# A hybrid decoder step on one Trainium2 core: rotary features 32 partitions apart, and seven low halves of weights made on GpSimd

## What is computed

```python
def rms_norm(x, w):
    y = xf * lax.rsqrt(jnp.mean(xf * xf, axis=-1, keepdims=True) + EPS)
    return (y * w.astype(jnp.float32)).astype(x.dtype)

def partial_rope(x, pos):
    half = ROT_DIM // 2
    ...
    x1, x2 = xf[..., :half], xf[..., half:ROT_DIM]
    out = jnp.concatenate([x1 * cos - x2 * sin, x2 * cos + x1 * sin, xf[..., ROT_DIM:]], axis=-1)
...
    aq = partial_rope(rms_norm(aq.reshape(B, S, ATT_HEADS, ATT_HD), q_norm_w), pos)
    ak = partial_rope(rms_norm(ak.reshape(B, S, ATT_HEADS, ATT_HD), k_norm_w), pos)
```

## Time and profile before

| | before |
|---|---|
| median of 3 runs | 477.11 us (476.24 to 478.72) |
| profiled execution, its own time | 477.14 us |
| its span in the trace | 475.0 us |
| PE busy | 462.9 us (97%), weight loads 422.3 us (89%) |
| DVE busy | 403.4 us (85%) |
| ACT busy | 290.2 us (61%) |
| POOL busy | 101.8 us (21%) |

### The profile page before, as it was taken

One profiled execution on the slowest core, in us unless ns is written; L12 is line 12 of the kernel. 1 busy time (PEld: TensorE's weight loads), 2 busy tenths in 40 slices (PEclk: granted clock), 3 DMA queues, 4 the chain that ended last, 5 costly groups with the idle time before them and its releaser, 6 DMA issues.

```text
span 475.0 us, 11339 instructions
## 1 busy us (share of the span) xinstructions
PE 462.9 (97%) x3860; PEld 422.3 (89%) x3860; DVE 403.4 (85%) x1650; ACT 290.2 (61%) x486; POOL 101.8 (21%) x181
## 2 busy tenths in 40 slices
PE   6999999999989999999999999999999999999997
PEld 4899899998779898888899889899898898899997
DVE  4898899699999898999899999789999954567861
ACT  4866545666964584994485695657848368334430
POOL 2031321013223223422321332312223110000000
PEclk9999999999999999999999999999999999999999
DMA  8697589657999999999999999998999996446511
GB/s 310 257 392 290 211 307 339 219 200 246 313 418 409 412 366 322 337 398 414 413 386 352 386 398 393 417 383 309 344 420 410 415 412 213 172 172 236 186 79 47
DMA packets 36665, 150.86 MB, mean 318 GB/s; under 512 B 5232, under 2 KB 6772, under 8 KB 29312
## 3 DMA queue, kind: packets, MB, share of 16 engines
q1 hardware_dynamic: 12304, 70.77, 39.2%
q0 software_dynamic: 19008, 67.20, 37.1%
q10 hardware_dynamic: 5296, 12.18, 6.6%
HBM read 137.37 MB, written 12.76 MB: 316 GB/s over the span
## 4 chain that ended last, share of the span: by engine, by line
PE 72%; DVE 12%; ACT 9%; issue 3%; DMA 3%; ACTq 0%; SPq 0%; DVEq 0%
PE pj L533 26%; PE pj L536 13%; PE wk L533 8%; PE pa L726 5%; PE wk L536 4%; DVE w L1056 3%; DVE kpages L1155 3%; ACT w L812 2%; DMA out_C_s<-cslot 2%; DVE cslot L1243 2%; ACT L832 2%; PE wk L486 2%; PE wk L638 2%; PE wk L670 1%; DMA cst<-in_consts 1%
## 5 line engine op out<-in xcount | busy, mean ns | idle before, releaser
L533 PE MATMUL pj<-xn,w 128*128 128x264 f32 x1328 | 180.9, 289 | 0.4 <-ACT mqT L965 0.4
L533 PEld LDWEIGHTS pj<-xn,w 128*128 128x128 f32 x1328 | 168.5, 189 | 8.5 <-issue 6.8
L1056 DVE TENSOR_TENSOR w<-wraw,w 128x1024 fp32r<-128x1024 f32 x112 | 136.9, 1226 | 11.0 <-ACT w L812 10.5
L812 ACT ACTIVATE w<-wraw 128x1024 fp32r<-128x1024 f32 x112 | 117.8, 1053 | 25.2 <-PE wk L536 12.8
L1155 DVE CUSTOM_DVE_ANT_0 kpages<-kpages,qbc 128x128 f32<-128x128 f32 x512 | 114.7, 288 | 1.6 <-DMA kpages<-in_cache_k 1.4
L536 PE MATMUL pj<-xn,w 128*128 128x264 f32 x664 | 94.2, 284 | 3.7 <-DVE w L1056 3.7
L536 PEld LDWEIGHTS pj<-xn,w 128*128 128x128 f32 x664 | 85.5, 188 | 4.6 <-DVE w L1056 4.6
L403 POOL DMA_DIRECT2D kpages<-in_cache_k x64 | 34.3, 536 | 178.4 <-DVE sco L1155 154.6
L403 POOL DMA_DIRECT2D vpages<-in_cache_v x64 | 33.9, 529 | 67.2 <-issue 37.3
L1155 DVE DVE_READ_ACCUMULATOR2_ANT sco<- 128x1 f32 x512 | 41.7, 81 | 0.0
L726 PE MATMUL pa<-vpages,prob 128*32 128x256 f32 x512 | 34.3, 385 | 0.8 <-ACT prob L870 0.8
(11 more groups left out here) (279 smaller groups left out, 658.3 us busy)
## 6 DMA issues: line engine op xcount, KB each, us to landing
wraw<-in_weights SPq DMA_DIRECT2D x56, 1024.0 KB, 7.9
kpages<-in_cache_k POOLq DMA_DIRECT2D x64, 512.0 KB, 8.0
vpages<-in_cache_v POOLq DMA_DIRECT2D x64, 512.0 KB, 10.3
cslot<-in_states SPq DMA_DIRECT2D x16, 512.0 KB, 10.5
out_C_s<-cslot ACTq DMA_DIRECT2D x16, 512.0 KB, 8.0
xres<-in_tokens SPq DMA_DIRECT2D x1, 1056.0 KB, 7.2
out_k_p<-kT ACTq DMA_DIRECT2D x4, 256.0 KB, 11.6
out_v_p<-v_nat ACTq DMA_DIRECT2D x4, 256.0 KB, 6.5
```

Of the source, the lines that this page charges most:

```text
L533: mm(bank[:, 0:T], w2[:, q, 0, k, :], src[:, g, k, :], start=(k == 0 and g == 0), stop=False)
L812: A(w2[:, n % WSPLIT, 0], wraw[:, pair % WRAW, :, (n % 2) * P:(n % 2 + 1) * P], ACT.Copy).then_inc(whi_ready, 1)
L1056: V.tensor_tensor(w2[:, q, 1], wraw[:, slot, :, half * P:(half + 1) * P], w2[:, q, 0], ALU.subtract).then_inc(wlo_ready, 1)
```

## The change

The features of a query or key head are put in another order by permuting columns of the weights, the norm weights and the outputs: features 0 to 15 and 16 others on partitions 0 to 31, features 16 to 31 and 16 others on partitions 32 to 63, the rest above. Cosine is 1 and sine 0 for the features that aren't rotated; the sine carries the sign. DVE then multiplies partitions 32 to 63 by the sine and writes the product to partitions 0 to 31, and the other way round. PE's product with `rot` goes. Query rows, which have to come out in the old order, are made by matmuls with a permutation matrix (`back`) in place of transposes. The low halves of chunks 1 to 7 are made by POOL, with a semaphore of their own. Before the decay rows POOL does a broadcast of 8 numbers whose result nobody uses.

```diff
+        def low_ready(n):
+            return (own_lo_ready, n) if 1 <= n <= OWN else (wlo_ready, 1 if n == 0 else n + 1 - OWN)
...
             def load_w(n):
                 if n >= WRAW:
-                    sp.wait_ge(wlo_ready, 2 * (n - WRAW + 1))
+                    for half in range(2):
+                        sp.wait_ge(*low_ready(2 * (n - WRAW) + half))
...
+            def split_lo(n):
+                pool.wait_ge(own_lo_ready, n - 1)
+                pool.wait_ge(whi_ready, n + 1)
+                pool.tensor_tensor(w2[:, n % WSPLIT, 1], wraw[:, (n // 2) % WRAW, :, (n % 2) * P:(n % 2 + 1) * P], w2[:, n % WSPLIT, 0],
+                                   ALU.subtract).then_inc(own_lo_ready, 1)
+
+            pool.wait_ge(blank, 6)
+            for n in range(1, 4):
+                split_lo(n)
             pool.wait_ge(proj, 2)
             for s in range(KSLOTS):
                 keys(s)
+            split_lo(4)
             for s in range(VSLOTS - 1):
                 values(s)
+            for n in range(5, OWN + 1):
+                split_lo(n)
+
+            pool.wait_ge(own_lo_ready, OWN)
+            nc.gpsimd.partition_broadcast(gm[:, 0, :], qmask[0:1, 0, 0:HEADS]).then_inc(blank, 1)
+            pool.wait_ge(blank, 7)
             pool.wait_ge(rows_ready, 1)
...
-                pe.wait_ge(wlo_ready, n + 1)
+                pe.wait_ge(*low_ready(n))
...
-            def norm_sums(ss, ro, i, src):
-                mm(ss[:, 0:T], ones, sq[:, i, :], start=True, stop=True)
-                mm(ro[:, 0:T], rot, src, start=True, stop=True).then_inc(norm_ps, 1)
+            def norm_sums(ss, i):
+                mm(ss[:, 0:T], ones, sq[:, i, :], start=True, stop=True).then_inc(norm_ps, 1)
...
                     pe.wait_ge(evac, g + 1)
-                    if g == 0:
-                        pe.wait_ge(boot_r, 16)
                     if g >= 2:
-                        pe.wait_ge(q_ready, g - 1)
+                        pe.wait_ge(rs_ready, g - 1)
...
-                    last = tr(bank[0:NB, (h - first) * P:(h - first + 1) * P], qT[:, h, SEQ:T], P)
+                    last = mm(bank[0:NB, (h - first) * P:(h - first + 1) * P], qT[:, h, SEQ:T], back, start=True, stop=True)
...
-                        pe.wait_ge(attg_ready, 2 * j)
...
-                        pe.wait_ge(mrs_ready, j + 1)
...
-            for n in range(1, AHEAD):
-                split_lo(n)
-            def rope_norm(x, r, ro, done):
-                ch.step(V.tensor_tensor(hT[:, 0, :], ro[:, 0:T], sin, ALU.mult))
-                ch.link(V.tensor_tensor(x, x, cos, ALU.mult))
-                ch.link(V.tensor_tensor(x, x, hT[:, 0, :], ALU.add))
+            def rope_norm(x, r, done):
+                low, high, both = slice(0, LO), slice(LO, 2 * LO), slice(0, 2 * LO)
+                ch.step(V.tensor_tensor(hT[low, 0, :], x[high], sin[high], ALU.mult))
+                ch.step(V.tensor_tensor(hT[high, 0, :], x[low], sin[low], ALU.mult))
+                ch.link(V.tensor_tensor(hT[both, 1, :], x[both], cos[both], ALU.mult))
+                ch.link(V.tensor_tensor(x[both], hT[both, 0, :], hT[both, 1, :], ALU.add))
                 V.tensor_tensor(x, x, r, ALU.mult).then_inc(done, 1)
             for h in range(HEADS):
-                if h + AHEAD < HEADS + LOW:
+                if OWN < h + AHEAD < HEADS + LOW:
                     split_lo(h + AHEAD)
...
-                dve.wait_ge(norm_ps, h + 1)
                 dve.wait_ge(rs_ready, h + 1)
...
+ORDER = np.concatenate([np.arange(ROT // 2), np.arange(ROT, ROT + LO - ROT // 2), np.arange(ROT // 2, ROT),
+                        np.arange(ROT + LO - ROT // 2, HD)])
...
+    c[np.arange(P), C_BACK + ORDER] = 1.0
```

More of the change, by code:

```diff
@@ L66 @@
 JOBS = 4
+OWN = HEADS - 1
 BLANKS = 6
 C_ID, C_ONE, C_EPS, C_PICK, C_PICKB, C_FIRST = 0, 128, 256, 257, 273, 288
-C_ROT, C_MASK, C_TRIT, C_COS, C_SIN, C_RANK, C_END = (
+C_BACK, C_MASK, C_TRIT, C_COS, C_SIN, C_RANK, C_END = (
     288, 416, 800, 928, 928 + T, 928 + 2 * T, 928 + 2 * T + 32)
@@ L237, in build @@
         ones = cst[:, C_ONE:C_ONE + P]
-        rot = cst[:, C_ROT:C_ROT + P]
+        back = cst[:, C_BACK:C_BACK + P]
         mask3 = cst[:, C_MASK:C_MASK + 384]
@@ L281, in build @@
         wload = [sem(f"wload{i}") for i in range(WRAW)]
-        whi_ready, wlo_ready = sem("whi_ready"), sem("wlo_ready")
+        whi_ready, wlo_ready, own_lo_ready = sem("whi_ready"), sem("wlo_ready"), sem("own_lo_ready")
+        def low_ready(n):
+            return (own_lo_ready, n) if 1 <= n <= OWN else (wlo_ready, 1 if n == 0 else n + 1 - OWN)
         kload = [sem(f"kload{i}") for i in range(KSLOTS)]
@@ L572, in keys_side @@
                         pe.wait_ge(c_ready, NB * j - 2) if j else pe.wait_ge(q_ready, HEADS)
[L573 removed]
                     else:
                         pe.wait_ge(c_ready, NB * j) if j else pe.wait_ge(qs_ready, 2)
[L576 to L577 removed]
+                    norm_sums(wk[2 * n], n)
                 if i in (4, 6):
@@ L1115, in _ @@
                 dve.wait_ge(boot_r, 16)
-                dve.wait_ge(norm_ps, h + 1)
                 dve.wait_ge(rs_ready, h + 1)
-                rope_norm(qT[:, h, :], rs[:, h % 2, :], wk[2 * (h % 2) + 1], q_ready)
+                rope_norm(qT[:, h, :], rs[:, h % 2, :], q_ready)
                 dve.wait_ge(q_ready, h + 1)
@@ L1203, in keys_side @@
                     n = i // 2 - 1
-                    dve.wait_ge(norm_ps, HEADS + 2 * j + n + 1)
                     dve.wait_ge(rs_ready, HEADS + 2 * j + n + 1)
                     dve.wait_ge(mlg_ready, j)
-                    rope_norm(kT[:, n, :], rs[:, n, :], wk[2 * n + 1], kT_ready)
+                    rope_norm(kT[:, n, :], rs[:, n, :], kT_ready)
                     dve.wait_ge(kT_ready, 2 * j + n + 1)
@@ L1435, in constants @@
     half = ROT // 2
-    for m in range(half):
-        c[m + half, C_ROT + m] = -1.0
-        c[m, C_ROT + m + half] = 1.0
+    c[np.arange(P), C_BACK + ORDER] = 1.0
     r = np.arange(P)
@@ L1448, in constants @@
     for s in range(2):
-        c[s * half:(s + 1) * half, C_COS:C_COS + T] = np.cos(ang)
-        c[s * half:(s + 1) * half, C_SIN:C_SIN + T] = np.sin(ang)
+        c[s * LO:s * LO + half, C_COS:C_COS + T] = np.cos(ang)
+        c[s * LO:s * LO + half, C_SIN:C_SIN + T] = np.sin(ang) * (1 - 2 * s)
     c[:, C_RANK:C_RANK + 32] = 2 * BIG * (TOPK - 0.5 - np.repeat(np.arange(NBLK)[::-1], HEADS))[None, :]
@@ L1467, in weight_pairs @@
 def weight_pairs(w_in, w_proj_mlstm, w_proj_attn, w_out):
-    cuts = [w_in[:, AQ + 256 * n:AQ + 256 * (n + 1)] for n in range(4)]
-    cuts += [w_in[:, g + 256 * j:g + 256 * (j + 1)] for j in range(JOBS) for g in GROUPS]
+    pair = np.concatenate([ORDER, HD + ORDER])
+    cuts = [w_in[:, AQ + 256 * n + pair] for n in range(4)]
+    cuts += [w_in[:, g + 256 * j + (pair if g == AK else np.arange(256))] for j in range(JOBS) for g in GROUPS]
     for w in (w_in[:, GA:GA + D], w_in[:, GM:GM + D], w_proj_mlstm, w_proj_attn, w_out):
@@ L1495 @@
         "consts": constants(),
-        "columns": np.concatenate([cols(n) for n in ("norm_w", "q_norm_w", "k_norm_w", "mh_norm_w")], axis=1),
+        "columns": np.concatenate([cols("norm_w"), cols("q_norm_w")[ORDER], cols("k_norm_w")[ORDER], cols("mh_norm_w")], axis=1),
         "tokens": np.concatenate([np.ascontiguousarray(inputs["x_prompt"])[0], np.ascontiguousarray(inputs["x_sample"])[:, 0]]).T
@@ L1513 @@
     y = g["y"].reshape(P, KC, T).transpose(2, 1, 0).reshape(T, D)
-    k_p = g["k_p"].transpose(3, 0, 2, 1).reshape(rows)
+    there = np.argsort(ORDER)
+    k_p = g["k_p"][:, there].transpose(3, 0, 2, 1).reshape(rows)
     v_p = g["v_p"].reshape(JOBS, P, 2, 256).transpose(2, 1, 0, 3).reshape(rows)
@@ L1520 @@
     return (y[:SEQ].reshape(1, SEQ, D), y[SEQ:].reshape(NB, 1, D), k_p, v_p, C_p, g["n_p"], g["m_p"].reshape(1, 1, MH),
-            by_sample(g["k_s"]), by_sample(g["v_s"]), C_s, n_s, g["m_s"])
+            by_sample(g["k_s"][there]), by_sample(g["v_s"]), C_s, n_s, g["m_s"])
```

3 lines of the change are left out of this document (1 added, 2 removed).

## The result

The changed kernel takes 494.35 us (median of 4 runs, 492.64 to 495.34), the kernel before 477.92 us in the same runs: ratio 1.0348 [1.0326, 1.037], **+16.4 us**. The forecast was +5.8 with a range up to 488. The direction was right, the size was not. The profiled execution takes 493.83 us, its span is 492.1 us.

A forecast was written before the change was run, and what follows sets the result against it. PE was taken to bound the kernel nearly everywhere, with DVE close behind. 477.14 us plus 6.0 for the heads stage minus 0.2 for the body gave 482.9 us (+1.2%), range 474.5 to 488.0.

The forecast's parts named there:

- PE's products with `rot`: Sixteen fp32 products of 0.45 us go from PE: 3.6 us in the heads stage, 3.6 us in the body.
- time taken off PE counts: Premise that PE bounds nearly everywhere, so its savings count where DVE or a late half doesn't take them back.
- DVE's rotation: Five DVE instructions per head: 2.09 us against 1.73, 0.36 more; upper end 2.3 us, 0.57 more.
- A low half on POOL: One low half made by POOL takes 2.2 us, against 1.22 on DVE; ends 0.95 and 2.65 us.
- When half 5 is there: Heads stage: POOL's half 5, behind the value loads, comes at 36.5 us; PE wants it at 32.6 and waits 3.9.
- POOL and DVE hold each other up: Start of the heads stage: POOL's first half holds DVE's `x_lo` once, making PE and all behind it 2.0 us later.
- The end of the heads stage: Half 7 ends at 42.9 us, last `q_ready` comes at 53.7, next chunk starts at 55.9 instead of 49.9: +6.0 us.
- Query rows: End of the heads stage: fp32 matmuls of 0.22 us replace eight transposes of 0.11 us, 0.9 us more.
- The decay rows: POOL's decay rows start at about 44 us, are spread at 50 to 52, needed at 58: no cost.
- The body: Rounds after the heads stage: -0.9 in round 0, +0.36 each in rounds 1 and 2, 0 in round 3; sum -0.2 us.
- more held up: Rival: POOL comes in twice at the start, halves take 2.65 us, or body rotations cost their upper end; 485 to 489, chance 0.18.

The follow-up runs named there:

- rotation alone: The changed kernel with all low halves back on DVE in the old places and no unused broadcast; 485.94 us, ratio 1.0184.
- unread product: The rotation alone with one fp32 product of 264 columns more on PE ahead of each sum of squares, 16 in all, unread; 487.01 us, ratio 1.02.
- the fills: The changed kernel with each of POOL's seven low halves replaced by three fills writing zeros, which read nothing; 488.64 us, ratio 1.0233.
- halves ahead of value loads: The changed kernel with POOL's low halves 4 to 7 all ahead of the loads of the value pages; 492.60 us, ratio 1.0317.
- POOL's code ahead of the casts: The changed kernel with one small subtraction on POOL, and a wait for its end, in front of POOL's casts; 492.88 us, ratio 1.0322.
- POOL's halves alone: The kernel before with low halves of chunks 1 to 7 and the unused broadcast on POOL, rotation unchanged; 483.16 us, ratio 1.0109.
- The variants with the same holds: Versions of the changed kernel that keep POOL's subtracting halves, with their order, an early subtraction or PE filler products changed; 492.44 to 493.11 us.

## Why the prediction was wrong

The direction was right, and for reasons that are in the sum: halves late on POOL, and DVE's chain behind them. The holds later in the stage and the low clock are not in it. By its own steps:

- **PE's products with `rot`**, 3.6 us in each stage: gone, as said, but in the heads stage the condition of "time taken off PE counts", that DVE doesn't take it back, wasn't met. DVE had 1.6 us of slack in 26 there, which the longer rotations alone used up (rotation alone; unread product).
- **DVE's rotation**: 2.09 taken, 2.29 measured, the upper end, for the reason that the page gave. The term was put only on the last four rotations and on the rounds; it counts eight times, +4.5 us on DVE.
- **A low half on POOL**: 2.2 taken, 2.40 measured. Good enough.
- **When half 5 is there**: ready at 36.5 forecast, 37.8 measured; a wait of 3.9 forecast, 2.5 measured (5.05 with the fills). Near, but it doesn't set the end (halves ahead of value loads), and the nearness is luck: with its 2.0 us for the hold the forecast has the first three halves done at 23.4 us, and they were at 26.04; the page loads then took 6.9 us of POOL's time and not 10.7.
- **POOL and DVE hold each other up**: mis-placed. The forecast priced the hold at `x_lo` alone, +2.0; there it was zero, since POOL's first half started at 18.76 us, 1.8 us after `x_lo` had ended, and where a subtraction did meet `x_lo` (POOL's code ahead of the casts) it was POOL that waited. A wait of 1.70 us came at chunk 1 instead, from the 11.1 us ahead of the first subtraction, which no step had.
- **The end of the heads stage is the step that failed.** POOL's half 7 was forecast to end at 42.9 and ended at 42.80. But the step assumed that DVE was up to date then, with four rotations and two low halves to go. The rule that had been applied at `x_lo` holds at every half that meets DVE at work: five holds, 10.4 us. At 43.1 DVE still had three instructions of head 2, the gates' rows, five rotations and the two low halves before it: 59.14 and not 53.7.
- **Query rows**: +0.9 forecast; 3.87 us in place of 1.23, so +2.6. The 0.9 is right at full clock; the rest is the low clock, a term that was absent.
- **The decay rows** cost nothing, as said, though they are spread at 59.8 to 61.3 us and not at 50 to 52: PE is still at the query rows then. With POOL's halves alone DVE did wait 1.4 us for them.
- **The body**: -0.2 forecast, +2.4 measured. By how late PE is, from round to round: +0.8 in the first chunk, at the low clock; -0.9 in round 0, as said; +1.2, +1.1 and +0.7 in the other three, forecast +0.4, +0.4 and 0; -0.6 in the merge. The three are near two rotations x 0.56 us each, so a start of a round is bound by DVE in all of them. The rise in the first chunk and the gain in the merge were in no step, and nearly cancel.

Of the rivals, "more held up" (485 to 489 us) came nearest. Of its three parts only the last was met, the body's rotations at their upper end; POOL didn't come in at the start, and a half took 2.40 us and not 2.65. It counted two holds, not five. What stays open: why the clock fell after a wait of 2.05 us in the second round of one run and not after 2.05 in the changed kernel; and why the last store of the changed kernel's profiled execution lands 1.5 us late. The variants with the same holds lie 1.2 to 1.9 us under the changed kernel (492.4 to 493.1), but in the traces their last DVE instruction starts at 487.6 to 488.5 us, about when its does (488.04), and what is shorter is the stretch behind it: 2.6 us in place of 4.1.

## What to carry to other kernels

Work that is moved to POOL and reads SBUF isn't beside DVE: price it as its duration, once for every half or tile that meets a DVE instruction which reads SBUF alone, and add that to DVE's stream, not only where the first meeting is. Before counting what is taken off the busiest engine, add up the second one's stream over the same stage and subtract its idle time; here 97% against 85% hid a stage in which they were 1.6 us apart. Several mechanisms of one price should be summed over all their places before one place is called the bound.
